# A fused two-block transformer kernel: the first norm's row scale moved behind its projections, and its input loaded in pieces

## The reference, cut to what matters

```
h = rmsnorm(x, norm_attn_g[l])      # x * rsqrt(mean(x*x) + 1e-6) * g, row by row
u = h @ w_in[l]                     # 1024 x 5632
u_q, u_k, u_v, u_pool, u_gate = jnp.split(u, splits, axis=-1)
q = rope_partial(...); k = rope_partial(...)
gates = jax.nn.sigmoid(u_gate.reshape(B, S, N_BRANCHES, D_MODEL))
```

## Time and profile before

| what | value |
|---|---|
| median of the runs | 891.46 us |
| the profiled execution's own time | 893.22 us |
| its span, first to last instruction | 891.4 us |
| PE busy | 835.6 us, 94% |
| DVE busy | 598.5 us, 67% |
| ACT busy | 449.6 us, 50% |
| POOL busy | 94.9 us, 11% |
| DMA | 142.94 MB, mean 160 GB/s |
| mean granted TensorE clock | 0.981 |

### The profile page before, as it was taken

One profiled execution on the slowest core, in us unless ns is written; L12 is line 12 of the kernel. 1 busy time (PEld: TensorE's weight loads), 2 busy tenths in 40 slices (PEclk: granted clock), 3 DMA queues, 4 the chain that ended last, 5 costly groups with the idle time before them and its releaser, 6 DMA issues.

```text
span 891.4 us, 13063 instructions
## 1 busy us (share of the span) xinstructions
PE 835.6 (94%) x5359; PEld 742.7 (83%) x5359; DVE 598.5 (67%) x942; ACT 449.6 (50%) x791; POOL 94.9 (11%) x105
## 2 busy tenths in 40 slices
PE   4998999889999999989998999999976999999897
PEld 3876887769999888879987798999765999999685
DVE  5777667766666745657568677746766589997543
ACT  4655556535555634364475446543465545554332
POOL 6000000000000000000300000000000255555000
PEclk9999999999999999999989999999999899999999
DMA  9644544454555555364754233235522355555451
GB/s 272 235 159 142 179 141 153 137 206 142 179 175 180 187 188 190 131 236 130 230 177 160 88 120 99 95 104 180 189 94 95 101 184 189 190 189 181 150 189 47
DMA packets 84939, 142.94 MB, mean 160 GB/s; under 512 B 4962, under 2 KB 43136, under 8 KB 84880
## 3 DMA queue, kind: packets, MB, share of 16 engines
q1 hardware_dynamic: 82704, 137.11, 47.2%
q0 software_dynamic: 2016, 4.93, 1.9%
q10 hardware_dynamic: 160, 0.07, 0.0%
HBM read 140.53 MB, written 1.05 MB: 159 GB/s over the span
## 4 chain that ended last, share of the span: by engine, by line
PE 66%; DVE 20%; ACT 7%; DMA 3%; issue 2%; POOL 0%; POOLq 0%; DVEq 0%; ACTq 0%
PE PS L1088 63%; DVE low_r L2039 10%; PE PS L1097 3%; ACT high L1613 2%; DVE WK_f L2047 2%; DMA low_f<-in_w_up_dram 2%; ACT WK_f L1610 2%; DVE AR_f L2039 1%; DVE AR_r L2039 1%; DVE AR_f L2047 1%; ACT AR_r L1613 1%; DMA low_f<-in_w_in_dram 1%; ACT XN L1610 1%; DMA low_f<-in_w_xq_dram 1%; DVE WK_f L2043 1%
## 5 line engine op out<-in xcount | busy, mean ns | idle before, releaser
L2039 DVE TENSOR_TENSOR low_r<-low_f,high 128x1024 fp32r<-128x1024 f32 x254 | 321.5, 1312 | 99.6 <-ACT high L1613 99.5
L1613 ACT ACTIVATE high<-low_f 128x1024 fp32r<-128x1024 f32 (+1 forms) x262 | 255.6, 1029 | 88.3 <-DMA low_f<-in_w_down_dram 40.3
L1088 PE MATMUL PS<-HTh,high 128*128 128x256 f32 x888 | 255.3, 288 | 1.8 <-DVE HTl_r L2039 1.8
L1088 PE MATMUL PS<-HTl_r,high 128*128 128x256 f32 x888 | 252.7, 285 | 0.0
L1088 PE MATMUL PS<-HTh,low_r 128*128 128x256 f32 x856 | 243.6, 285 | 0.0
L1088 PE MATMUL PS<-high,AR_r 128*128 128x512 f32 (+1 forms) x656 | 197.5, 384 | 4.8 <-DVE low_r L2039 2.5
L1088 PEld LDWEIGHTS PS<-HTh,high 128*128 128x128 f32 x888 | 171.5, 193 | 3.7 <-issue 2.8
L1088 PEld LDWEIGHTS PS<-HTl_r,high 128*128 128x128 f32 x888 | 171.4, 193 | 0.1
L1088 PEld LDWEIGHTS PS<-HTh,low_r 128*128 128x128 f32 x856 | 165.1, 193 | 0.0
L1088 PEld LDWEIGHTS PS<-high,AR_r 128*128 128x128 f32 (+1 forms) x656 | 119.7, 185 | 29.9 <-issue 5.2
L1088 PE MATMUL PS<-low_r,AR_r 128*128 128x512 f32 (+1 forms) x328 | 124.3, 381 | 0.0
(11 more groups left out here) (173 smaller groups left out, 847.7 us busy)
## 6 DMA issues: line engine op xcount, KB each, us to landing
low_f<-in_w_in_dram SPq DMA_DIRECT2D x41, 1024.0 KB, 5.2
low_f<-in_w_up_dram SPq DMA_DIRECT2D x38, 1024.0 KB, 5.1
low_f<-in_w_down_dram SPq DMA_DIRECT2D x27, 1024.0 KB, 4.9
low_f<-in_w_out_dram SPq DMA_DIRECT2D x8, 1024.0 KB, 5.0
low_f<-in_w_xkv_dram SPq DMA_DIRECT2D x4, 1024.0 KB, 5.6
low_f<-in_w_branch_gla_dram SPq DMA_DIRECT2D x2, 1024.0 KB, 5.8
low_f<-in_w_branch_nsa_dram SPq DMA_DIRECT2D x2, 1024.0 KB, 5.0
low_f<-in_w_xq_dram SPq DMA_DIRECT2D x2, 1024.0 KB, 5.3
```

Of the source, the lines that this page charges most:

```text
L1088: return nc.tensor.matmul(o, l, r, start=start, stop=stop, skip_group_check=True)
L1613: return nc.scalar.activation(o, i, ACT.Copy, bias=0.0, scale=1.0)
L2039: return nc.vector.tensor_tensor(o, a, b, op)
```

## The change

The rows of x are no longer scaled ahead of the transposes. TensorE turns x itself, and the root of each row is applied when the five projections that read this `HT` leave PSUM (q, k, v, pool, gate): as the scale operand of ACT's copy or tanh, or as a multiplication on DVE in place of its copy. For the gate, whose tanh takes half of the value, a second root with a quarter of the factor is taken (`half_root`). The rotation by `rope` goes on in PSUM, on unscaled values. x is loaded in four pieces of 256 KB and unit 0 in two of 512 KB, and SP issues them in the order x(0,0), x(1,0), first half of unit 0, x(0,1), x(1,1), second half of unit 0, unit 1. The order of the first steps is new (`first_turns`), the constants of the angles move to the first piece of `cst`, `positions` moves to the head of POOL's queue, `angles` moves ahead of q on DVE and the sine is a step of its own, and in k's projection the transpose of q's first rows stands one step later.

```
+    def first_turns(self):
+        for g in range(2):
+            for i in range(2):
+                self.turn_ht(0, i, g, "X", self.big)
+            for i in range(2):
+                self.step("split_hi", u=g, parts=(i,))
+                self.turn_lo(0, i, g)
+                self.step("split_lo", u=g, parts=(i,))
+            for i in range(2):
+                self.step(("first_squares", "first_roots")[g], i=i)
+        self.step("angles")
+        self.n_split = self.n_low = 2
...
-        for i in range(2):
-            self.step("rms", i=i, src="x")
-            self.step("scaled", stage=0, i=i)
-        for i, g in ((0, 0), (0, 1), (1, 0), (1, 1)):
-            self.turn_ht(0, i, g, "XN", self.big)
-            self.turn_lo(0, i, g)
-            if (i, g) == (0, 0):
-                self.ahead(1)
-            else:
-                self.lows()
-        self.ahead(2)
+        self.first_turns()
         first = self.wide("q", 0, evac=True)
-        for _ in range(2):
-            next(first)
-        self.step("angles")
+        next(first)
+        self.step("sines")
         self.all(first)
...
-        self.all(self.turns("q", "qT", 0, self.qbank, self.wide("k", 0, evac=True)))
+        self.all(self.turns("q", "qT", 0, self.qbank, self.wide("k", 0, evac=True), (2, 1)))
...
+            def first_squares(s):
+                i = s["i"]
+                for j in range(2):
+                    act.wait_ge(s_x[i][j], 16)
+                    m = squares(i, j)
+                m.then_inc(s_xsq, 1)
+            def first_roots(s):
+                i = s["i"]
+                act.wait_ge(s_xinv, i + 1)
+                fn(half_root(i), st[:, 4 * i + 2:4 * i + 3], ACT.Sqrt, scale=256.0)
+                fn(root(i), st[:, 4 * i + 2:4 * i + 3], ACT.Sqrt, scale=1024.0).then_inc(s_xrt, 1)
...
+                if key in RAW:
+                    act.wait_ge(s_xrt, s["i"] + 1)
                 if key == "gate":
                     act.wait_ge(*use.full)
                     fn(GT[:, s["i"], 512 * s["j"]:512 * s["j"] + 512], bank(use), ACT.Tanh,
-                       scale=0.5).then_inc(use.read[0], 1)
+                       scale=half_root(s["i"])).then_inc(use.read[0], 1)
...
+                    if key in RAW and use.eng == "act":
+                        act.wait_ge(*use.full)
+                        fn(copied(s), bank(use), ACT.Copy, scale=root(s["i"])).then_inc(use.read[0], 1)
...
+                elif key in RAW and use.eng == "dve":
+                    dve.wait_ge(s_xrt, i + 1)
+                    dve.wait_ge(*use.full)
+                    ts(copied(s), bank(use), root(i), None, ALU.mult).then_inc(use.read[0], 1)
...
-            for i in range(2):
-                nc.sync.dma_start(X[:, i, :], xd[:, i, :]).then_inc(s_x[i], 16)
-            load(0)
+            first = S.plan[0][3][0][1]
+            for j in range(2):
+                for i in range(2):
+                    h = slice(512 * j, 512 * j + 512)
+                    nc.sync.dma_start(X[:, i, h], xd[:, i, h]).then_inc(s_x[i][j], 16)
+                w0 = v3(low[0][0][:], 4, 512)[:, 2 * j:2 * j + 2]
+                nc.sync.dma_start(w0, first[:, 2 * j:2 * j + 2]).then_inc(loaded[0] if j else s_w0, 16)
             load(1)
```

More of the change, by code:

```diff
@@ L32 @@
 _at = 0
[L33 to L34 removed]
+for _name, _width in (("ident", 128), ("freq", 8), ("cm", 256), ("dist", 384), ("cdist", 30), ("cmask", 30), ("up", 128),
+                      ("un", 128), ("reset", 256)):
     CONST[_name] = (_at, _width)
@@ L275, in lows @@
         while self.n_low < self.n_split:
-            self.step("split_lo", u=self.n_low)
+            self.step("split_lo", u=self.n_low, parts=(0, 1))
             self.n_low += 1
@@ L281, in ahead @@
             self.lows()
-            self.step("split_hi", u=self.n_split)
+            self.step("split_hi", u=self.n_split, parts=(0, 1))
             self.n_split += 1
@@ L470, in given, with turns @@
             yield
-    def turns(self, key, name, g, bank, fill):
+    def turns(self, key, name, g, bank, fill, lead=(1, 1)):
         for i in range(2):
-            next(fill)
-            yield
+            for _ in range(lead[i]):
+                next(fill)
+                yield
             bank((name, i, g), True)
@@ L981, in two_blocks @@
         own_act, own_dve, own_pool = sem("own_act"), sem("own_dve"), sem("own_pool")
-        s_x = [sem("load_x0"), sem("load_x1")]
+        s_x = [[sem(f"load_x{i}{j}") for j in range(2)] for i in range(2)]
+        s_w0 = sem("load_unit0")
         s_id, s_g0, s_cst, s_vr, s_pos, s_lam = (sem("load_" + n) for n in ("id", "g0", "cst", "vr", "pos", "lam"))
@@ L1140, in turn_ht @@
                 else:
-                    pe.wait_ge(*U[RESIDUAL[stage], i, g].read)
+                    if stage == 0:
+                        pe.wait_ge(s_x[i][g], 16)
+                    else:
+                        pe.wait_ge(*U[RESIDUAL[stage], i, g].read)
                     src = X
@@ L1623, in split_hi @@
                 half, slot = K * n // 2, u % NSLOT
-                act.wait_ge(loaded[slot], load_count[u])
+                if u == 0 and 0 in s["parts"]:
+                    act.wait_ge(s_w0, 16)
+                else:
+                    act.wait_ge(loaded[slot], load_count[u])
                 if u >= NSLOT:
@@ L1633, in split_hi @@
                     return
-                for o in (0, half):
-                    cp(high[slot][:, o:o + half], low[slot][0][:, o:o + half]).then_inc(s_hi, 1)
+                for q in s["parts"]:
+                    h = slice(half * q, half * q + half)
+                    cp(high[slot][:, h], low[slot][0][:, h]).then_inc(s_hi, 1)
             def warm(s):
@@ L1647, in rms @@
                 for j in range(2):
[L1648 to L1651, removed]
+                    act.wait_ge(*U[{"x4": "xo", "x5": "down2"}[src], i, j].read)
                     m = squares(i, j)
@@ L1721, in x3_read, with sines @@
                         act.wait_ge(*U["out2", i, j].read)
-            def angles(s):
+            def sines(s):
                 act.wait_ge(s_angle, 1)
@@ L2071, in split_lo @@
                     return
-                for q, o in enumerate((0, half)):
+                for q in s["parts"]:
+                    h = slice(half * q, half * q + half)
                     dve.wait_ge(s_hi, 2 * u + q + 1)
-                    tt(r[:, o:o + half], f[:, o:o + half], high[slot][:, o:o + half], ALU.subtract).then_inc(s_lo, 1)
+                    tt(r[:, h], f[:, h], high[slot][:, h], ALU.subtract).then_inc(s_lo, 1)
             def gain0(s):
```

41 lines of the change are left out of this document (27 added, 14 removed).

## The result

Over 19 runs of each, the changed kernel takes 895.6 us (median; 892.77 to 899.25) and the kernel before 892.25 (888.35 to 900.15). The ratio is 1.0038, 95% interval 1.0022 to 1.0054: **slower by about 3.4 us**, where 887.3 (a gain of 4.2) was forecast. It is within 1%, and outside the range given.

What follows compares the result with a forecast made beforehand. PE, busy 94%, was taken to bound the kernel, its start at 15.43 set by an ACT and DVE chain. Start -4.2, clock, slacks, scales and positions 0 each, from the 891.46 median: 887.3 us, range 885.0 to 890.5.

Steps and rivals of the forecast that it cites:

- Does the lead survive?: From q's end through k: units 2 and 3 land at 22.2 and 27.1 again, so PE keeps its 4.2 us.
- Moving `positions`: Front of POOL's queue: its 256 tiny pieces beside x's first pieces cost 0, bound +0.7 us.
- The 174 GB/s from 15 to 20 us: DMA rate in the old profile, pulled down by POOL's small loads ahead of unit 2's landing.
- the weights come late (slower): Rival at unit 2's landing: decides at a slip of 4.5 us; 895 us at a slip of 6; chance 0.04.
- the four thin slacks of 0.2 to 0.7 us: Between q's end and k's end: slacks of 0.3, 0.5, 0.7, 0.2 us, none negative; cost 0, bound +1.0.
- The start: First projection matmul: at 11.2 instead of 15.43, 4.2 us earlier, as the norm leaves the chain.
- The end of q: PE's q projection: ends at 24.6, from 11.2 + 13.5, and wants unit 2's first half at 24.7.
- Fixed costs in series: Rival at the first loads: each DMA's fixed cost adds up, unit 0's second half at 23.6; 900.5 us; chance 0.01.
- own range: Forecast case for the whole kernel: 886.0 to 889.2 us around 887.3.
- The slow pace at the start: PE's first projection matmuls: 1.2 GHz for 4.9 us again, bounds 3.4 to 6.4, so 0 with ±0.75 us.
- The evacuations with a scale: Projection results leaving PSUM on ACT and DVE: 0 extra cost; bound +0.7 us on the chain.
- The moved transpose: q's first rows during k's projection: turning them one step later avoids a 2.2 us PE wait, keeping the lead.

Runs made afterwards that it cites:

- e11_before_pos_first: Kernel before, with only the load of `positions` moved to the head of POOL's queue; 893.39 us, one run.
- e2_pos_back: Changed kernel with the load of `positions` back in its old place, behind the twelve loads of `VR`; 893.13 us, 1.0008 of the kernel before.
- e9_defer_rows: Changed kernel with POOL's four repeated rows (`subg`, `glag`, `gateb`, `pool_scale`) held until PE has done k; 888.13 us, 0.9934 of the kernel before.
- e4_x_whole: Changed kernel with x loaded in two whole pieces, both ahead of unit 0; 895.44 us, 1.0036 of the kernel before.
- e7_lead1: Changed kernel with POOL's nine last small loads held until k is done, constants behind unit 3, moved transpose taken back; 888.0 us, 0.9950 of the kernel before.
- e12_after_again: Changed kernel as it is, traced a second time; 899.16 us, one run.
- e15_defer_short: Changed kernel with only the three short repeated rows (`subg`, `glag`, `gateb`) held until k is done; 888.74 us, 0.9978 of the kernel before.

## Why the prediction was wrong

**The step that failed** is in "Does the lead survive?": "they will land there again: the bytes in front of them are the same". The bytes were; the time of the DMA engines wasn't. Unit 2 came at 26.8 (25.6 in the second trace) and not at 22.2. Two things in the working led there.
- The loads at the start were taken to stream as before, and "Moving `positions`" stood at 0 with a bound of 0.7. The stream lost 1.4 us by 8 us, some 0.8 of it to `positions` (1.1 where it was moved alone, in e11_before_pos_first: more than the bound). Already at the start it shows: x's second two pieces landed at 8.7 and 9.4, forecast 7.1 and 7.8, and unit 0's second half at 11.0, forecast 9.2. Unit 1 was forecast unchanged at 11.9 and landed at 13.9.
- The 174 GB/s from 15 to 20 us were read, and taken as a constant of the place. They were a cost in engine time that unit 2 had to sit through. A delay in front of it seems to grow and not to be passed on one to one: 1.1 us of hole became 2.1 in e11_before_pos_first, and some 0.8 less of it gave 2.0 to 3.2 back in e2_pos_back. With landings that scatter by 1.2 us the factor is not measured.

**The rival that came true** is "the weights come late (slower)", at 0.04. Its place, unit 2's landing behind POOL's small loads, was right, and its time of 895 us, worked out for a slip of 6 us, came out at 895.6. That the two agree is in part luck: the slip was 4.6 us in one trace (k began at 29.25 against 29.10) and 3.4 in the other. What made the kernel slower was the clock, put at 2.1 us and measured at 2.4 and 3.0. And the rival left the clock out of its threshold: it was said to decide at a slip of 4.5 us, but a slip of 1.4 in e2_pos_back already takes the whole gain (1.0008, 3.25 us of idle and 7.33 us for k's first 24 matmuls). The mechanism was written down and its chance set too low: the four thin slacks of 0.2 to 0.7 us were all weighed for ACT and DVE, and the one input all of them share, the landing, wasn't given a spread.

**What held.**
- The start: forecast 11.2, measured 10.38 in one trace and 10.29 in the other. The norm was the chain. It came 0.8 sooner as the identity and the gain arrived at 4.36 instead of 5.23 and the first two pieces of x at 3.8 and 4.8, so the first two banks were turned by 6.5.
- The end of q: forecast 24.6, measured 24.07.
- The lead carries through if the weights are there: 5.15 us at 95 us in e9_defer_rows, and a ratio of 0.9934 (medians 4.2 us apart on that chip). The sum of slacks in the prediction was not disproved.
- Fixed costs in series are out: the second half of unit 0, put at 23.6 by that rival, landed at 11.0, and e4_x_whole with two DMAs fewer has the same rate. The section that the prediction cites there (the Trainium skill, DMA: Bandwidth & Descriptors, "Anatomy of one DMA") measures loads that GpSimd issues; these come from SP.

**What was off but didn't decide.** The bounds of the sum, added up, give 886.5 to 890.4 around 887.3; the forecast's "own range" of 886.0 to 889.2 doesn't follow from them. The slow pace at the start was put at 4.9 us; full pace came at 13.79, 3.4 us after the first projection matmul, worth 0.75 us at half price. PE had done 16 transposes in two groups by its start at 10.38, with 2.27 us of idle between them. The evacuations with a scale cost more than the 0 they were put at. Groups by form, 25 to 130 us, of the changed kernel (busy, mean ns):

```profile
L1625 ACT ACTIVATE AR_f<-PS,st 128x512 f32<-128x512 f32 x13 | 8.9, 685 | 17.3 <-DVE PS L2077 11.3 <-PE PS L1103 3.8 <-issue 2.1
L1631 ACT ACTIVATE AR_f<-PS 128x512 f32<-128x512 f32 x5 | 2.9, 584 | 0.0
L2081 DVE TENSOR_SCALAR AR_f<-PS,st 128x512 f32<-128x512 f32 x3 | 2.3, 752 | 2.8 <-PE PS L1103 2.8
L2088 DVE COPY AR_f<-PS 128x512 f32<-128x512 f32 x3 | 2.1, 688 | 1.0 <-PE PS L1112 1.0
```

0.10 us more for one on ACT, 0.06 on DVE. In e9_defer_rows the lead at 95 us is whole, so there it was off the path. The moved transpose, of which the prediction said that it "is what keeps the lead", isn't, at least with early weights: e7_lead1 goes without it at the same time. The 2.2 us wait it was to prevent was computed for a unit 3 at 27.1, and with early weights its split begins at 23.72. In the changed kernel as it is, no run takes the step back.

**What stays open.** The difference of medians is 3.35 us, of which 2.7 are seen by 95 us, 2.1 in the second trace. The rest is in later stretches, where the slow and fast levels of PE's clock fall differently; that is argued, no run isolates it. e4_x_whole and e12_after_again show how far single executions stray (spans of 890.0 and 897.3 at about the same lateness by 95 us). Why a short row read for 128 partitions holds an engine so long, and whether `subg`, `glag` or `gateb` does more of it, wasn't tried apart; nor what the four rows of `lamv`, repeated in the same way, take (the microsecond from 14 to 15 is at 130 GB/s in e9_defer_rows, with a share of 0.89); nor what in the new order of the first loads makes its own hole at 5 us.

## What to carry to other kernels

A head start is worth what the next input allows: before counting it through, write down for the first wait behind it how late its data may come, and what shares the DMA engines with it. Read the DMA's share and its rate side by side: a share near 1.00 at a rate of 80 to 140 GB/s, where 400 is usual, is a load that costs engine time and not bytes, and everything queued beside it pays for that. Rows repeated for 128 partitions and four-byte pieces belong behind the first weights, which here is one wait on POOL's queue. The wait moves their cost to another place, so hold back only these, and look at what they meet there: with the five small weights (0.6 MB) held as well, PE paid 1 us at 56 us.

## What the runs showed of the hardware

- Three loads of 140 KB together, short rows repeated over 128 partitions, keep the whole core's DMA at 72 to 99 GB/s from 15 to 21 us of the changed kernel; a packet of POOL's queue took 0.74 us of an engine there (16 to 20 us), 0.09 in e9_defer_rows, where they were absent. Almost alone, from 42 to 44 us of e15_defer_short, it took 0.56. The Trainium skill, DMA: Bandwidth & Descriptors, in "Queues, rings and completion order", says that each engine goes round between its queues packet by packet; the trace agrees in kind, since from 16 to 20 us SP's queue, with 1 MB units to move, gets 108 packets through beside POOL's 65, and 17% of the time beside 75%.
- A load of 256 pieces of 4 bytes at the head of POOL's queue took the rate of a microsecond from 392 to 137 GB/s.
- After an idle time of 5.2 us PE is at 1.2 GHz (granted clock 0.50 from 28 to 32 us) until 34.07, 4.8 us after it began again: 11 matmuls at 0.43 instead of 0.23 us. In the second trace, after 4.3 us of idle, it lasts from 28.07 to 33.76.
